# Expert loop of a mixture-of-experts block: branch for a third block around each whole expert, panels given back product by product, third products interleaved, third results stored by ScalarE

## The reference

```
def hier_moe(xn, ...):            # 512 tokens, D = 1024
    g_idx = argmax(group logits)                # top-1 of 4 groups
    top_v, top_i = top_k(expert logits, 2)      # top-2 of the group's 8 experts
    wts = g_prob * softmax(top_v)
    # for each of 32 experts e, for the tokens that chose it:
    h = silu(xb @ w_gate[e]) * (xb @ w_up[e])   # 1024 -> 512
    out = h @ w_down[e]                         # 512 -> 1024
    y[token] += out * wt
```

## Time and profile before

| | us |
|---|---|
| median of 3 runs | 1532.05 |
| lowest, highest | 1529.07, 1536.29 |
| the profiled execution, its own time | 1529.32 |
| its span, first to last instruction | 1527.6 |
| PE busy | 1406.1 (92%) |
| DVE busy | 702.0 (46%) |
| ACT busy | 486.6 (32%) |

### The profile page before, as it was taken

The page is one execution under the profiler, slowest core; times in us unless marked ns, Lnnn a source line. Parts: engine busy times, 40 slices in busy tenths (PEclk is TensorE's granted clock), DMA queues, the critical chain, the costliest instruction groups (busy, mean ns, idle before and its releaser), DMA issues.

```text
span 1527.6 us, 17831 instructions
## 1 busy us (share of the span) xinstructions
PE 1406.1 (92%) x6818; PEld 973.4 (64%) x6818; DVE 702.0 (46%) x1282; ACT 486.6 (32%) x727; POOL 39.5 (3%) x73
## 2 busy tenths in 40 slices
PE   6999995899988888999739999999999999999997
PEld 5877774444433343343217888778888888888886
DVE  4478647321110111010067656456255666666555
ACT  6462435001100010111054222325344444444552
POOL 2000000000000000000020010000000000000000
PEclk9999898899999999999969999999999999999999
DMA  9827335399999997899986553212312112212201
GB/s 358 345 107 275 115 138 220 144 426 427 427 424 429 424 428 318 360 427 424 428 292 265 217 210 123 81 56 85 111 56 107 59 56 87 79 56 81 86 15 56
DMA packets 36806, 336.80 MB, mean 220 GB/s; under 512 B 4560, under 2 KB 4688, under 8 KB 18384
## 3 DMA queue, kind: packets, MB, share of 16 engines
q1 hardware_dynamic: 29632, 304.69, 49.3%
q0 software_dynamic: 6624, 29.89, 5.5%
q10 hardware_dynamic: 432, 0.60, 0.1%
HBM read 312.62 MB, written 22.54 MB: 219 GB/s over the span
## 4 chain that ended last, share of the span: by engine, by line
PE 47%; DMA 2%; DVE 1%; ACT 1%; issue 0%; POOL 0%; SPq 0%; POOLq 0%; ACTq 0%; PEld 0%; PEldq 0%; DVEq 0%
PE ps L335 46%; DMA ring<-in_wts_dram 2%; PE ps L814 1%; DVE hres L1935 0%; DMA ar<-y_scratch,rt 0%; POOL ar L2270 0%; DVE ar L1943 0%; PE ps L777 0%; DVE ar L2046 0%; DMA y_scratch<-gate 0%; PE ps L341 0%; DVE hres L2049 0%; DVE ar L2193 0%; ACT ar L983 0%; ACT b_NH L1249 0%
## 5 line engine op out<-in xcount | busy, mean ns | idle before, releaser
L335 PE MATMUL ps<-ar 128*64 128x512 f32 (+5 forms) x814 | 172.1, 487 | 25.4 <-issue 7.5
L335 PE MATMUL ps<-ring,ar 128*64 128x512 f32 x784 | 178.3, 600 | 16.5 <-DMA ring<-in_wts_dram 8.3
L1814 DVE TENSOR_TENSOR ar<-ar,ps 128x256 f32<-128x256 f32 x34 | 14.3, 421 | 371.2 <-ACT ar L1125 368.7
L335 PE MATMUL ps<-b_NH,b_WH 128*128 128x512 f32 x688 | 178.0, 397 | 0.8 <-ACT b_NH L989 0.8
L335 PE MATMUL ps<-b_NH,b_WL 128*128 128x512 f32 x688 | 172.4, 389 | 0.0
L335 PE MATMUL ps<-b_NL,b_WH 128*128 128x512 f32 x688 | 170.1, 389 | 0.0
L1385 DVE TENSOR_TENSOR b_WL<-ring,b_WH 128x1024 fp32r<-128x1024 f32 x106 | 129.5, 1221 | 73.9 <-ACT b_WH L935 73.9
L935 ACT ACTIVATE b_WH<-ring 128x1024 fp32r<-128x1024 f32 x106 | 112.1, 1058 | 123.2 <-PE ps L335 122.3
L335 PEld LDWEIGHTS ps<-ar 128*64 128x64 f32 (+3 forms) x814 | 79.5, 162 | 110.1 <-issue 91.8
L335 PEld LDWEIGHTS ps<-b_NH,b_WL 128*128 128x128 f32 x688 | 129.2, 188 | 27.1
L335 PEld LDWEIGHTS ps<-b_NL,b_WH 128*128 128x128 f32 x688 | 129.1, 188 | 26.8
(11 more groups left out here) (306 smaller groups left out, 1900.6 us busy)
## 6 DMA issues: line engine op xcount, KB each, us to landing
ring<-in_wts_dram SPq DMA_DIRECT2D x83, 2048.0 KB, 16.9
ar<-in_wts_dram SPq DMA_DIRECT2D x25, 2048.0 KB, 27.9
spare<-in_wts_dram SPq DMA_DIRECT2D x24, 2048.0 KB, 27.0
ring<-in_wmod_dram SPq DMA_DIRECT2D x24, 512.0 KB, 4.8
ar<-in_wmod_dram POOLq DMA_DIRECT2D x24, 512.0 KB, 4.0
y_scratch<-gate POOLq DMA_DIRECT2D x11, 1024.0 KB, 21.2
y_scratch<-gate SPq DMA_DIRECT2D x44, 128.0 KB, 26.5
y_scratch<-ar SPq DMA_DIRECT2D x24, 128.0 KB, 24.5
```

Source lines behind the costliest of these rows:

```text
L335: return pe.matmul(o, l, m, start=start, stop=stop, skip_group_check=True)
L1814: return dve.tensor_tensor(h.rearrange("p (a c) -> p a c", a=2), g_.rearrange("p (a c) -> p a c", a=2), ps[:, b, :].rearrange("p (a g c) - ...
```

## The change

PE's branch is moved ahead of everything that belongs to expert n. In the path without a third block the order of the products is as it was; the increments in place of the third block (`no_third`) now stand ahead of them. In the path with one, the third block's products are put between the main ones. t_up is split into t_ua (half 0) and t_up (half 1), and SP waits for t_ua where it gives back a panel (n, 0). The third result is stored by ACT through its own DMA queue. DVE writes xT3 before the main block's `gated`.

```diff
-                landed(ua)
-                pe.wait_ge(S["m_xt"], 4 * g + 4 if n else 2)
-                if n:
-                    pe.wait_ge(S["m_hh"], n)
-                up(xTn, 2, panel(ua), 0).then_inc(S["m_ua"], 1)
-                if n:
-                    down_main(n - 1)
...
-                landed(ub)
-                up(xTn, 2, panel(ub), 1).then_inc(S["m_up"], 1)
+            def main_up(n, half):
+                g, i = n // 4, turn_of[n, half]
+                xTn = xTg[g % 2][:, :, 64 * (n % 4):64 * (n % 4) + 64]
+                landed(i)
+                if not half:
+                    pe.wait_ge(S["m_xt"], 4 * g + 4 if n else 2)
+                    if n:
+                        pe.wait_ge(S["m_hh"], n)
+                up(xTn, 2, panel(i), half).then_inc(S[("m_ua", "m_up")[half]], 1)
+            def third_pick(n):
+                if n:
+                    pe.wait_ge(S["t_y"], n)
...
+                pe.wait_ge(S["m_xt"], min(4 + n, NE))
+                pe.wait_ge(S["t_oh"], n + 1)
+                pick_third(0).then_inc(S["t_gx"], 1)
+            def third_up(n, half):
+                if not half:
+                    pe.wait_ge(S["t_xt"], n + 1)
+                up(xT3, 0, panel(turn_of[n, half]), half).then_inc(S[("t_ua", "t_up")[half]], 1)
+            def no_third(n):
+                for v in ("t_gx", "t_tx", "t_ua", "t_up", "t_d1", "t_d2"):
+                    if n:
+                        pe.wait_ge(S[v], n)
+                    pe.sem_inc(S[v], 1)
...
                 with pe.If(third(n)):
...
+                    third_pick(n)
                     if n:
...
+                        main_up(n, 0)
...
+                    third_turn(n)
+                    if n:
+                        down_main(n - 1)
+                    third_up(n, 0)
+                    if n:
+                        main_up(n, 1)
+                    third_up(n, 1)
                     main_pick(n)
...
                     main_turn(n)
...
+                    third_down(n)
                 with pe.Else():
+                    no_third(n)
                     if n:
...
+                        main_up(n, 0)
+                        down_main(n - 1)
+                    main_up(n, 1)
                     main_pick(n)
                     main_turn(n)
```

ScalarE, in the branch with a third block:

```diff
+                    third_rows(n)
+                    if n:
+                        result(n - 1)
+                    main_silu(n)
+                    third_silu(n)
+                    main_h(n)
+                    third_result(n)
+                    act.wait_ge(S["t_y"], n + 1)
+                    for q in range(2):
+                        act.dma_start(y_d[(NE + n) * CAP:(NE + n + 1) * CAP, 512 * q:512 * q + 512],
+                                      ysb3[64 * q:64 * q + 64, :]).then_inc(S["ty"], 16)
```

SyncE:

```diff
                         sp.wait_ge(S[("m_ua", "m_up", "m_d2")[m]], n + 1)
-                        sp.wait_ge(S["t_d2" if m == 2 else "t_up"], n + 1)
+                        sp.wait_ge(S[("t_ua", "t_up", "t_d2")[m]], n + 1)
...
-                if m == 1:
-                    with sp.If(third(n)):
-                        sp.wait_ge(S["t_y"], n + 1)
-                        store(NE + n, ysb3, "ty")
```

More of the change, by code:

```diff
@@ L36 @@
 xh xl hb hs std m_e m_oh m_gx m_xt m_ua m_up m_sg m_hh m_d1 m_ht m_d2 m_y y0 y1 y2
-t_e t_oh t_gx t_xg t_tx t_xt t_up t_sg t_hh t_d1 t_ht t_d2 t_y ty
+t_e t_oh t_gx t_xg t_tx t_xt t_ua t_up t_sg t_hh t_d1 t_ht t_d2 t_y ty
 v_w0 v_w1
@@ L665, in main_turn, with third_turn, third_down @@
                 turn_h(hh, 4).then_inc(S["m_d1"], 1)
-            for n in range(NE):
-                g, (ua, ub, dn) = n // 4, (turn_of[n, m] for m in range(3))
-                xTn = xTg[g % 2][:, :, 64 * (n % 4):64 * (n % 4) + 64]
-                landed(ua)
-                pe.wait_ge(S["m_xt"], 4 * g + 4 if n else 2)
-                if n:
-                    pe.wait_ge(S["m_hh"], n)
-                up(xTn, 2, panel(ua), 0).then_inc(S["m_ua"], 1)
-                if n:
-                    down_main(n - 1)
-                else:
+            def main_up(n, half):
[10 more added lines that the diff above has]
+                    pe.wait_ge(S["t_y"], n)
+                if n > N_MOD:
+                    pe.wait_ge(S["mpd"], 5)
+                pe.wait_ge(S["m_xt"], min(4 + n, NE))
+                pe.wait_ge(S["t_oh"], n + 1)
+                pick_third(0).then_inc(S["t_gx"], 1)
+            def third_turn(n):
+                pe.wait_ge(S["t_xg"], n + 1)
+                turn_third(6).then_inc(S["t_tx"], 1)
+            def third_up(n, half):
+                if not half:
+                    pe.wait_ge(S["t_xt"], n + 1)
+                up(xT3, 0, panel(turn_of[n, half]), half).then_inc(S[("t_ua", "t_up")[half]], 1)
+            def third_down(n):
+                i = turn_of[n, 2]
+                pe.wait_ge(S["t_hh"], n + 1)
+                turn_h(hh3, 6).then_inc(S["t_d1"], 1)
+                pe.wait_ge(S["t_ht"], n + 1)
+                landed(i)
+                down(hT3, 1, panel(i)).then_inc(S["t_d2"], 1)
+            def no_third(n):
[3 more added lines that the diff above has]
+                    pe.sem_inc(S[v], 1)
+            for n in range(NE):
+                if n == 0:
+                    main_up(0, 0)
                     for u in range(2, 4):
@@ L682, in tensor_program @@
                     pe.wait_ge(S["m_xt"], 4)
-                landed(ub)
-                up(xTn, 2, panel(ub), 1).then_inc(S["m_up"], 1)
                 with pe.If(third(n)):
+                    third_pick(n)
                     if n:
[L687 to L692, removed]
+                        main_up(n, 0)
+                    else:
+                        main_up(n, 1)
[6 more added lines that the diff above has]
+                    third_up(n, 1)
                     main_pick(n)
-                    pe.wait_ge(S["t_xg"], n + 1)
-                    turn_third(6).then_inc(S["t_tx"], 1)
                     main_turn(n)
[L697 to L704, removed]
+                    third_down(n)
                 with pe.Else():
+                    no_third(n)
                     if n:
[L707 to L710, removed]
+                        main_up(n, 0)
+                        down_main(n - 1)
+                    main_up(n, 1)
                     main_pick(n)
@@ L1152, in scalar_program, with main_silu @@
             n_over, third = read_ctl(act)
-            for n in range(NE):
-                if n:
-                    result(n - 1)
+            def main_silu(n):
                 act.wait_ge(S["m_up"], n + 1)
@@ L1159, in scalar_program, with main_h @@
                 silu_gate(sg, 2).then_inc(S["m_sg"], 1)
+            def main_h(n):
+                act.wait_ge(S["m_d1"], n + 1)
+                copy_h(hT, 4).then_inc(S["m_ht"], 1)
+            for n in range(NE):
                 with act.If(third(n)):
@@ L1177, in scalar_program @@
                     with act.If(n_over > j):
-                        third_block(NE + j)
+                        third_rows(NE + j)
+                        third_silu(NE + j)
+                        third_result(NE + j)
             hi(P_C0, 0)
@@ L1885, in vector_program @@
                     third_places(n, NE * CAP + CAP * n)
+                    third_turned(n)
                 with dve.Else():
@@ L1896, in vector_program @@
                 with dve.If(third(n)):
-                    third_block(n)
+                    third_gated(n)
                 with dve.Else():
                     if n:
[L1900 to L1903, removed]
+                        dve.wait_ge(S["t_hh"], n)
+                    dve.sem_inc(S["t_hh"], 1)
                 if n + 4 < NE:
@@ L2320, in sync_program @@
             sp.wait_ge(S["ctl"], 1)
-            n_over, third = read_ctl(sp)
+            n_over, _ = read_ctl(sp)
             def store(b, y, sem):
```

25 lines of the change are left out of this document (15 added, 10 removed).

## The result

The changed kernel takes 1585.4 us (median of 4 runs, 1584.71 to 1588.46) against 1532.09 us before. The ratio is 1.0347, 95% interval 1.0331 to 1.0363: slower by 53 us. The prediction was 1517.

A forecast was written before the change was run, and what follows sets the result against it. The expert loop was taken to end when the weight panels have landed, with PE following. Gains of 3.7 and 10.9 us sum to 14.6: 1529.32 becomes 1514.7, plus 2.7 for the runs' median is 1517.4, said as 1517; range 1511 to 1527.

The forecast's parts named there:

- What bounds the kernel: Expert loop: it ends when the weight panels have landed, PE follows; closing two idle DMA stretches gains at most 19.2 us.
- the 19.2: Expert loop: all there is to gain, from 4.75 us idle DMA in 296 to 301 and 14.5 in 597 to 618.
- The first hole: DMA idle at 296 to 301 us: earlier release of panel (1, 0) gains 3.7 us, bounds nothing and 4.75.
- The second hole, step by step: DMA idle in 597 to 618, experts 19 to 21: earlier panel releases close 11.5 of 14.5 us.
- the store: Third result of expert 20 on ACT's queue: two 128 KB transfers take 1.2 us, so PE's wait for xT3 goes.
- The rival with 18.8 us for it: Third store no faster on ACT's queue, xT3 of expert 20 at 606.4: 1528 us, chance 0.10.
- the jump ... stays inside and costs 0.32 us as before: PE's branch over the third block: the longer jump fits PE's room of 2048 instructions and costs 0.32 us.
- The 1153 ns row: Longest of 34 PE jumps over one third block before the change; median 320 ns; cited against the longer jump missing.
- the rival at 1525: PE's branches in the expert loop cost 1.15 us each, the longest near row: 1525 us, chance 0.11.
- The rival "slower": The longer jump misses its fetch, 5.81 us between any two experts, 30 times: about 1655 us, chance 0.04.
- From 1.5 us more at each the kernel is no faster: End of the expert loop: PE has some 14 us of slack over 10 branches, used up by 1.5 us more each.
- Whether PE keeps up: Experts 21 to 31: exposed branches show 0.3 or 0.85 us; last half 1 starts at 753.6, limiting the gain to 10.9.

The follow-up runs named there:

- the fastest run: The changed kernel with short branches around the third block's pieces, the first behind the expert's first product, main products standing once outside: 1515.59 us, ratio 0.9887.
- the two faster versions: The changed kernel with branch and third block only at experts 19 and 20: 1516.64 us; with short branches, the first behind the first product: 1515.59 us.

## Why the prediction was wrong

- **What bounds the kernel**: right. The end of the loop follows the landings; with the branches out of the way, closing the holes gave 15 to 18 us of the 19.2.
- **The first hole**: right in kind, too large in size for this change. The load was to go 3.7 us earlier, near 297. SyncE's release alone brought it to 297.94 (and 4.6 us of time, with 1.8 to 6.0 open). With PE's branch interleaved as in the change, but without a stall, it went at 299.25 (no branches) and 298.79 (short jumps), and at 300.07 in the fastest run. In the changed kernel itself the hole was lost to expert 1's stall of 6.41 us, and the load went at 306.55.
- **The second hole, step by step**: right, with one term mis-sized. The waits for DVE, the slower matmuls behind the first of them, the store on ACT's queue and the lengths of both experts are in the trace. From the start of the third picks of 19 to the end of its third down, 584.6 to 614.9 is 30.3 us; forecast 555.5 to 585.7, 30.2. The term: the store was put at 1.2 us on its own queue, and it took 7.3 to 11.0 beside a full DMA. That this cost almost nothing was luck: in the run without branches xT3 came just as PE's product ahead of it ended. The rival with 18.8 us for it was wrong too.
- **The step that failed: "the jump ... stays inside and costs 0.32 us as before".** It came from a row for a shorter jump (191 instructions) carried over to a longer one (288), and from the room of 2048 instructions that the Trainium skill gives PE (Runtime: NRT & Kernel Launch, Instruction fetch mechanics). The runs put 5.7 to 6.7 us in its place at seven of the 30 experts without a third block (2.5 and 3.7 us at two more), and PE waited 56.4 us behind line 707. They show no room of 2048: jumps of 257 to 288 instructions stall. The same section of the Trainium skill also says in a note that the instruction memory is only two lines of 16 KiB. Of the two statements the runs bear out this one. The prediction used only the first. Even the second would not have been enough: what counts is not only whether the target lies within two blocks but whether the second has arrived.
- **The 1153 ns row** was the sign. One of the 34 branches had already taken 3.6 times the median, and it ended 1.40 us after a fetch packet, as the long ones do. I used it as a price for all branches (the rival at 1525) and not as the short end of a stall of 6 us.
- **The rival "slower"** had the mechanism and was given 0.04. Its size (every jump stalls, 1655) was wrong too: about one in three did, branches and landings counted, since it depends on where the branch lies in its block.
- **"From 1.5 us more at each the kernel is no faster"** has the direction and not the size. 56.4 us behind line 707 over the 30 experts is 1.9 us each; by the rule, which counts the last ten, that makes the kernel some 4 us slower, and it became 53 slower. The stalls came in lumps of 6 us that PE's slack before 553 didn't cover: the third picks of expert 19 came 29 us late, and the holes opened again.
- **Whether PE keeps up**: in the run with short jumps ahead of the products the gaps behind the last transposes are 1.3 us each, where I had 0.85, and two of the three products behind them ran at the lower clock for most of their length (5.35 us for 16 matmuls instead of 3.65, 8.61 for 32 instead of 7.09). My estimate from these rows, 3 x 0.45 + 1.7 + 1.5 = 4.6 us, is most of the 5 to 6 us between it and the two faster versions; no run tests it alone.

## What to carry to other kernels

A branch costs by what it jumps over, and by what is queued ahead of it. Before code is put into a conditional, count the instructions of the part that is jumped over, and keep it well under a block of 256, or cut it into short branches around the pieces with the common work outside; put the branch behind work that is long enough to hide it: one product of 3.5 us hid only about half of a stall. In a view of grouped instructions read the maximum of a branch and not only its median: a single long one says that the fetch is near its edge. If the trace has the fetches as a queue of their own, lay their ends beside the ends of the long branches; here that pointed straight at the cause.

## What the runs showed of the hardware

- PE's instructions are fetched by packets of 16,384 bytes that pass through the same DMA engines as the weights and take 0.9 to 2.3 us. From 865 to 1547 us in the kernel after, 255 instruction records of PE lie between two fetches in the mean.
- On PE a branch that isn't taken took 65 to 94 ns. Behind jumps of 0.17 to 0.25 us the next fetch came at any distance, so they stayed in their block. Behind those of 0.28 us and more it began 3.0 to 4.8 us after their end where the DMA was full (all but one of 233 in the ten traces, which had 1.0), so they had left it. Of these, the ones that found their block there took 0.28 to 0.44 us, the others up to 6.7.
- The wait grows with the DMA's load. Where the DMA's share was under 0.65, the next fetch packet began 0.7 to 2.2 us after a branch had left its block. At the end of the loop (share 0.03 in 805 to 810) the packet for the branch at 805.40 began 1.0 us after it, and the branch took 3.72 us; for the one at 360.62, with the DMA full, it was 4.1 us and 6.67.
- The stall needs no branch: experts 1 and 18 of the kernel after have gaps of 6.41 and 4.95 us behind branches of 0.41 and 0.34. At expert 18 the fetch packet ended at 566.24 and PE's product began at 567.61, again 1.4 us later. By the count, both jumps land a few instructions ahead of a block's end.
- The nine gaps of 4.2 to 6.9 us on PE in the kernel after were each followed by a product at the lower level of the clock (1.2 of 2.4 GHz) for most of its length. At expert 5 the granted clock was 0.58 from 368 to 374 and 1.00 from 374 to 378, and the product took 5.95 us instead of 3.6. So a stall of 6 us costs about 8. The length of the gap alone doesn't decide it: after 2.88 us at expert 15 the clock stayed at 1.00 (524 to 529), and in the run with short jumps one gap of 1.29 us was followed by 5.35 us for 16 matmuls and one of 1.30 by the full clock.
- Two 128 KB stores on a queue of their own landed in 7.3 to 11.0 us beside a full queue of 2 MB loads (the run with the store alone, share 1.00, and the fastest run), and in 4.1 to 5.7 us where the DMA's share was 0.7. Behind five such loads on their queue it was 18.8 us.
